# A stick-breaking attention whose joins move to GpSimd and whose value products change operands

## The reference

```python
proj = _rms(x, norm_g) @ w_in            # 1024 x 2048
q, g = split(proj)                       # 16 heads of 64
for each tile i of 128 queries, each head:
    z = q @ k.T / 8                      # masked to keys before the query
    a = exp(log_sigmoid(z) + reverse exclusive cumsum of log_sigmoid(-z))
    o = a @ v                            # 128 x 64
o = o * silu(g)
return x + o @ w_out
```

## Time and profile before

| | |
|---|---|
| median of 3 runs | 2390.4 us (2380.78 to 2392.75) |
| the profiled execution: its time | 2385.55 us |
| its span, first to last instruction | 2383.7 us |
| busy share PE, PEld, DVE, ACT, POOL | 97%, 52%, 67%, 43%, 9% |
| granted TensorE clock, mean | 0.997 of 2.4 GHz |
| second attention (first scan of query tile 0 to last value product) | 1980.8 to 2280.2 us |
| output product behind it | 2284.3 to 2383.7 us |

### The profile page before, as it was taken

One profiled execution on the slowest core, in us unless ns is written; L12 is line 12 of the kernel. 1 busy time (PEld: TensorE's weight loads), 2 busy tenths in 40 slices (PEclk: granted clock), 3 DMA queues, 4 the chain that ended last, 5 costly groups with the idle time before them and its releaser, 6 DMA issues.

```text
span 2383.7 us, 30315 instructions
## 1 busy us (share of the span) xinstructions
PE 2301.2 (97%) x12762; PEld 1234.2 (52%) x12762; DVE 1592.2 (67%) x2053; ACT 1017.9 (43%) x1482; POOL 208.1 (9%) x254
## 2 busy tenths in 40 slices
PE   7999999999999999999999988999999999989999
PEld 5445444444444444445544456654444446777765
DVE  6888867866766666787632389965534406989961
ACT  6255334322323223433322587732313216888841
POOL 0001030000000001623301100022000000000000
PEclk9999999999999999999999999999999999999999
DMA  5111010111110212103111000111231200010021
GB/s 187 36 37 69 1 36 36 61 46 71 58 49 36 71 71 71 38 1 142 36 71 36 32 5 1 62 46 36 71 141 36 72 1 1 1 36 1 1 89 54
DMA packets 50488, 116.02 MB, mean 49 GB/s; under 512 B 2418, under 2 KB 8107, under 8 KB 49968
## 3 DMA queue, kind: packets, MB, share of 16 engines
q1 hardware_dynamic: 48616, 105.40, 12.4%
q10 hardware_dynamic: 1736, 8.68, 0.9%
HBM read 101.49 MB, written 12.58 MB: 48 GB/s over the span
## 4 chain that ended last, share of the span: by engine, by line
PE 80%; DVE 11%; ACT 6%; issue 1%; DMA 1%; SPq 0%; DVEq 0%; ACTq 0%
PE PS L72 76%; PE PS L75 4%; ACT RG L81 3%; DVE R L93 2%; DVE RG L107 2%; ACT OV L84 2%; DVE R L101 1%; DVE RG L104 1%; DVE RG L101 1%; DVE RG L93 1%; ACT R L81 1%; DMA RG<-in_a_w_in 1%; DVE oss L110 1%; DVE dg L104 1%; DVE scl L110 0%
## 5 line engine op out<-in xcount | busy, mean ns | idle before, releaser
L72 PE MATMUL PS<-R,RG 128*128 128x512 f16 (+1 forms) x5184 | 1104.2, 374 | 9.4 <-DVE R L101 4.2
L72 PEld LDWEIGHTS PS<-R,RG 128*128 128x128 f16 (+1 forms) x5184 | 514.0, 104 | 592.8 <-issue 10.9
L72 PE MATMUL PS<-RG,R 128*128 128x512 f16 (+1 forms) x2904 | 631.2, 377 | 2.0 <-DVE R L101 1.7
L72 PEld LDWEIGHTS PS<-RG,R 128*128 128x128 f16 x2904 | 283.7, 98 | 330.0 <-issue 2.9
L81 ACT ACTIVATE RG<-RG,scl 128x4096 f16<-128x4096 f32 (+2 forms) x70 | 177.9, 2557 | 199.5 <-DVE scl L113 199.5
L101 DVE SCALAR_TENSOR_TENSOR RG<-RG,scl 128x4096 f16<-128x4096 f32 (+2 forms) x70 | 213.1, 3051 | 71.5 <-ACT RG L81 71.5
L101 DVE SCALAR_TENSOR_TENSOR R<-PS,scl,R 128x512 f32<-128x512 f32 (+1 forms) x227 | 159.2, 742 | 121.2 <-PE PS L72 98.8
L81 ACT ACTIVATE R<-PS,scl 128x512 f32<-128x512 f32 (+1 forms) x128 | 83.5, 685 | 326.4 <-PE PS L72 287.0
L107 DVE TENSOR_TENSOR_SCAN RG<-RG 128x127 f32<-128x127 f32 (+7 forms) x128 | 168.4, 1343 | 76.3 <-ACT RG L81 76.1
L110 DVE TENSOR_REDUCE scl<-RG 128x1 f32<-128x4096 f32 (+1 forms) x35 | 150.3, 4293 | 98.9 <-DMA RG<-in_w_ff 41.1
L72 PE MATMUL PS<-R,OV 128*128 128x64 f32 (+2 forms) x1456 | 193.7, 274 | 5.7 <-DVE R L93 5.4
(11 more groups left out here) (137 smaller groups left out, 1667.2 us busy)
## 6 DMA issues: line engine op xcount, KB each, us to landing
RG<-in_w_ff SPq DMA_DIRECT2D x16, 2048.0 KB, 8.5
RG<-in_a_w_in SPq DMA_DIRECT2D x8, 2048.0 KB, 8.7
xspill<-R ACTq DMA_DIRECT2D x2, 4096.0 KB, 16.0
RG<-in_w_kv SPq DMA_DIRECT2D x4, 2048.0 KB, 8.2
RG<-in_b_w_in SPq DMA_DIRECT2D x4, 2048.0 KB, 8.1
RG<-in_w_in SPq DMA_DIRECT2D x3, 2048.0 KB, 8.2
R<-in_x SPq DMA_DIRECT2D x8, 512.0 KB, 8.0
RG<-in_w_out SPq DMA_DIRECT2D x2, 2048.0 KB, 7.8
```

The lines of the kernel that those rows point to most:

```text
L72: return self.engine.matmul(*a, **k) if self.engine else Nothing()
```

## The change

- **Joins.** `tensor_tensor` of kept and beta moves from DVE's queue to POOL's, behind a new signal `scanned`; POOL no longer all-reduces the gates' peaks.
- **Value products.** V2 becomes stationary (64 columns), AT2 moving (128 columns). The result has features on partitions, odd heads on partitions 64 to 127, in the layout the output product wants of its stationary operand.
- **Gates.** All sixteen gate products become `product_t`, in the order `G2`; the last two, of tile 39, stay inside the attention.
- **Gate transposes** fall away: `gate_high` and `gate_low` read the gated values in SBUF (`gated_at`) and write HG, in the place of Q2. The bound of query tiles 0 to 6 comes from one PE matmul with ones (`gate_bound`) at u = N-1, that of tile 7 from another at (c, t) = (0, 1); splits of tiles 0 and 1 are issued inside the last steps of the attention.
- **Buffers.** `eb(u)` is in the raw buffer for u < 2, then in slot 0, so sigmoid of z waits for the peak of tile 40 at u = 0 and for the last gate product at u = 2. Tile 40 is loaded a second time, and its pieces move to u = 26 to 33. OUT moves to R2.

```diff
-        EB = [WS[:, 1024 * i:1024 * i + 1024] for i in range(4)]
+        def eb(u):
+            at = 1024 * u if u < 2 else 4096 + 1024 * (u % 4)
+            return RG[:, at:at + 1024]
         def kept(u):
-            return EB[2 + u] if u < 2 else EC[u % 3]
+            return EC[u % 3]
+        def gated_at(i, g):
+            return GATED[i // 4].rearrange("p (k t q) -> p k t q", k=8, t=4)[:, 4 * g:4 * g + 4, i % 4, :]
+        G2 = [("g2", c, mi, n) for n in range(2) for c in range(2) for mi in range(4)]
-        OUT = [R3[:, 1024 * i:1024 * i + 1024] for i in range(8)]
+        OUT = [R2[:, 1024 * i:1024 * i + 1024] for i in range(8)]
-        sb_pieces = range(22, 30)
+        sb_pieces = range(26, 34)
...
 # tensor
-            for t in range(NT - 1):
-                for c in range(2):
-                    product_n(38 + c, t, ("g2", t, c), bank=6 + c if t == NT - 2 else None)
+            for z, key in enumerate(G2[:14]):
+                _, c, mi, n = key
+                product_t(38 + c, mi, n, h_rhs, key, bank=z - 6 if z >= 12 else None)
+            def gate_bound(first, last, bank):
+                key = ("gate_bound", first)
+                b = banks.take_at(key, bank)
+                e.wait_ge(*sig("g_peak").at(last - 1))
+                e.wait_ge(*banks.free(key))
+                e.matmul(b[:, first:last], ones[:, :], col(24 + first, last - first), start=True,
+                         stop=True).then_inc(*full.up(*key))
...
-                            mm = e.matmul(banks.ap(("pvb", i, g))[:, 64 * (h % 8):64 * (h % 8) + 64],
-                                          AT2[v % 2][:, at:at + 128], V2[:, j, 64 * h:64 * h + 64],
-                                          start=(j == 0), stop=(j == i))
+                            r, q = 64 * (h % 2), 128 * (h % 8 // 2)
+                            mm = e.matmul(banks.ap(("pvb", i, g))[r:r + 64, q:q + 128], V2[:, j, 64 * h:64 * h + 64],
+                                          AT2[v % 2][:, at:at + 128], start=(j == 0), stop=(j == i))
...
-            gate_turn(0)
-            gate_turn(1)
             for c in range(2):
                 for t in range(NT):
+                    if (c, t) == (0, 1):
+                        gate_bound(7, 8, 7)
...
-                    e.wait_ge(*sig("bank_dve").at("gt", t, 1))
+                    e.wait_ge(*sig("g_low").at(t))
...
-                    if c == 0 and t + 2 < NT:
-                        gate_turn(t + 2)
 # vector
-                    scan.then_inc(*step.up())
-                if u < N:
-                    i, hs = sb_groups[u]
-                    w = width(i)
-                    eb, ec = by_head(EB[u % 4], u)[:, :, 0:w - 1], by_head(kept(u), u)[:, :, 1:w]
-                    e.wait_ge(*sig("beta").at(u))
-                    e.wait_ge(*step.last())
-                    e.tensor_tensor(eb, eb, ec, ALU.mult).then_inc(*sig("joined_b").up(u))
+                    scan.then_inc(*sig("scanned").up(u))
...
+                if u == N:
+                    gate_factors(0, 7)
+                    gate_low(0)
+                    gate_low(1)
 # scalar
                 if u < N:
-                    if u in (2, 3):
-                        e.wait_ge(*sig("joined_b").at(u - 2))
-                    if u >= 4:
+                    if u == 0:
+                        e.wait_ge(*sig("w_factor").at(40))
+                    if u == 2:
+                        e.wait_ge(*full.at(*G2[15]))
+                    if u >= 6:
                         e.wait_ge(*full.at("tb", u - 4, 1))
...
 # gpsimd
-            for i in range(NT):
-                e.wait_ge(*sig("g_peak").at(i))
-                across(col(32 + i), col(24 + i)).then_inc(*sig("g_top").up(i))
+            for u, (i, hs) in enumerate(sb_groups):
+                w = width(i)
+                beta, left = by_head(eb(u), u)[:, :, 0:w - 1], by_head(kept(u), u)[:, :, 1:w]
+                e.wait_ge(*sig("scanned").at(u))
+                e.wait_ge(*sig("beta").at(u))
+                e.tensor_tensor(beta, beta, left, ALU.mult).then_inc(*sig("joined_b").up(u))
             measure(41)
 # sync
-            for i in range(32, 42):
+            for i in range(32, 41):
                 load(i)
+            e.wait_ge(*sig("bank_full").at("tb", 1, 1))
+            e.dma_start(w_raw(40).rearrange("p (k n) -> p k n", k=8), w_source(40)).then_inc(
+                *sig("raw_again").up(by=16))
+            load(41)
```

More of the change, by code:

```diff
@@ L274, in tile_slot @@
                 return 2
[L275 removed]
+            return i % 3 if i < 40 else 41 - i
         def w_slot(i):
@@ L1014, in tensor @@
                     product_t(36 + c, mi, n, h_rhs, ("q2", c, mi, n), ready=h_ready("b_norm_2", n))
-            for t in range(NT - 1):
-                for c in range(2):
-                    product_n(38 + c, t, ("g2", t, c), bank=6 + c if t == NT - 2 else None)
-            def gate_turn(i):
-                for g in range(2):
-                    b = banks.take(("gt", i, g))
-                    e.wait_ge(*sig("g_gated").at(i, g))
-                    e.wait_ge(*banks.free(("gt", i, g)))
-                    for k in range(4):
-                        at = 512 * g + 128 * k
-                        mm = e.transpose(b[:, 128 * k:128 * k + 128], GG[:, i, at:at + 128], ident[:, :])
-                    mm.then_inc(*full.up("gt", i, g))
+            for z, key in enumerate(G2[:14]):
[8 more added lines that the diff above has]
+                         stop=True).then_inc(*full.up(*key))
             e.wait_ge(*sig("constants").at("mask_s"))
@@ L1067, in tensor @@
             scores([1])
-            product_n(38, NT - 1, ("g2", NT - 1, 0), bank=6)
+            product_t(39, 2, 1, h_rhs, G2[14], bank=6)
             scores([2])
-            product_n(39, NT - 1, ("g2", NT - 1, 1), bank=7)
+            product_t(39, 3, 1, h_rhs, G2[15], bank=7)
             for u in range(1, N + 2):
@@ L2063, in gate_low, with gate_factors @@
             def gate_low(i):
+                e.wait_ge(*sig("g_high").at(i, 1))
                 for g in range(2):
-                    key = ("gt", i, g)
-                    e.wait_ge(*sig("g_high").at(i, g))
-                    low_half(HT[:, i, g, 0, :, :], HT[:, i, g, 1, :, :],
-                             banks.ap(key).rearrange("p (k q) -> p k q", k=4), col(40 + i)).then_inc(
-                        *banks.empty([key], sig("bank_dve"), *key))
-            def gate_factor(i):
-                e.wait_ge(*sig("g_top").at(i))
-                power(col(63 + i), col(40 + i), col(32 + i)).then_inc(*sig("g_factor").up(i))
+                    up = sig("g_low").up(i) if g else step.up()
+                    low_half(HG[:, i, g, 0, :, :], HG[:, i, g, 1, :, :], gated_at(i, g), col(40 + i)).then_inc(*up)
+            def gate_factors(first, last):
+                key, n = ("gate_bound", first), last - first
+                e.wait_ge(*full.at(*key))
+                power(col(63 + first, n), col(40 + first, n), banks.ap(key)[:, first:last], key=key).then_inc(
+                    *sig("g_factor").up(first))
             N = len(sb_groups)
@@ L2118, in vector @@
                         *(sig("weight").up(40) if u - 1 == sb_pieces[-1] else step.up()))
-            for i in range(2):
-                gate_factor(i)
-                gate_low(i)
+                if u == N:
+                    gate_factors(0, 7)
+                    gate_low(0)
+                    gate_low(1)
             for c in range(2):
@@ L2734, in scalar, with gate @@
             e.dma_start(OV[:, 2048:2176], A["c_ms"]).then_inc(*sig("mask_in").up(by=16))
-            def gate_silu(t):
-                for c in range(2):
-                    key = ("g2", t, c)
-                    e.wait_ge(*full.at("g2", t, 1))
-                    e.wait_ge(*sig("w_scale").at(38 + c, 0))
-                    e.activation(GG[:, t, cols512(c)], banks.ap(key), ACT.Silu, scale=w_scale(38 + c)).then_inc(
-                        *banks.empty([key], sig("bank_act"), *key))
-            for t in range(NT - 1):
-                gate_silu(t)
+            def gate(key, function):
+                _, c, mi, n = key
+                e.wait_ge(*full.at(*key))
+                e.wait_ge(*sig("w_scale").at(38 + c, 0))
+                return e.activation(GT[n][:, 512 * (4 * c + mi):512 * (4 * c + mi) + 512], banks.ap(key), function,
+                                    scale=w_scale(38 + c))
+            for key in G2[:14]:
+                gate(key, ACT.Silu).then_inc(*banks.empty([key], sig("bank_act"), *key))
             def gate_high(i):
-                e.wait_ge(*sig("g_factor").at(i))
-                e.wait_ge(*full.at("gt", i, 1))
+                e.wait_ge(*sig("g_factor").at(0 if i < 7 else 7))
+                e.wait_ge(*full.at("zb", N - 1))
                 for g in range(2):
-                    key = ("gt", i, g)
-                    e.activation(HT[:, i, g, 0, :, :], banks.ap(key).rearrange("p (k q) -> p k q", k=4),
```

(4 more changed lines are left out.)

64 lines of the change are left out of this document (35 added, 29 removed).

## The result

The changed kernel takes 2413.18 us, median of 4 runs (2411.69 to 2414.72), beside 2390.66 for the kernel before in the same rounds: ratio 1.0102, 95% interval 1.0074 to 1.0131. It is slower, and the forecast of 2417 lies 4 us off. The profiled execution has a span of 2412.9 us, 29.2 more than before's 2383.7 (the forecast was +26.7), at the same mean granted clock, 0.997.

What follows compares the result with a forecast made beforehand. VectorE's queue, together with TensorE, was taken to set the pace from tile 2. Terms 27.2 + 8 + 1.1 + 1.1 - 10.7 = +26.7 on a median of 2390.4 give 2417 us; own range 2402 to 2446, stated range 2370 to 2446.

Steps and rivals of the forecast that it cites:

- Exclusion of scan and join: Attention: a VectorE scan with two SBUF sources and a GpSimd join block each other, so the pace is scan plus join.
- 27.2 floor: Attention, tiles 2 to 7: scan plus join sums to 292.2 against 265.0 us, +27.2 if the shared resource never idles.
- 8 idling: Attention: idle time of the resource shared by scan and join, taken as 3%, +8 us, bounds 0 and +24.
- 1.1 for the last join: End of the attention: the last join lies bare, 2.35 us for 1.22, +1.1 us.
- each less 0.14: Attention: with exclusion, scan and join each take their own length less 0.14 us.
- 4.8 for the low halves: Tiles 4 and 5: tile 40's 8 low halves, also with two SBUF sources, 8 x 0.60 = 4.8 us.
- Value products as nothing: TensorE, attention: 0 to 20 us gain from cheaper records against 33 us of shape changes; taken as 0, bounds -5 and +10.
- The tail, -10.7: Behind the attention: earlier start -3.6, fewer transposes -4.4, no wait at t = 6 -2.7; together -10.7 us, bounds -7 and -12.
- The wait at t = 6: Output stage: the product of t = 6 no longer waits 3.1 us behind tile 41's low half; -2.7 us.
- ScalarE's wait at u = 2, +1.1: Start of the attention: sigmoid of z waits for the last gate product, one sigmoid later; +1.1 us, 0 to 1.1.
- side by side: Rival, attention: scan and join overlap freely, since the scan holds nothing GpSimd needs; -21.5 us, 2369; chance 0.16.
- Side by side with the changes of shape: Rival, attention: scan and join overlap, but 128x64 shape changes make TensorE the bound; 2402 us; chance 0.10.

Runs made afterwards that it cites:

- e5: The changed kernel with each scan replaced by two reduces of the same columns with one SBUF source; 2397.99 us, ratio 1.0051.
- e1: The changed kernel with the joins alone put back on VectorE, 128x64 value products kept; 2393.81 us, ratio 1.0042.
- e6: The changed kernel with joins on VectorE and both heads' values as the 128x128 stationary operand; 2380.66 us, ratio 0.9972.
- e3: The changed kernel with the value products of the kernel before, joins still on GpSimd; 2426.79 us, ratio 1.0175.
- e12: The changed kernel with the old value products and one needless matmul per group ahead of the wait for the join; 2413.89 us, ratio 1.0127.
- e11: The changed kernel with joins on VectorE, odd heads first with 128x128 value products, tile 7's bound one product later; 2384.31 us, ratio 0.9994.
- e7: The changed kernel with the old value products and two needless matmuls per half group ahead of the wait for the join; 2440.81 us, ratio 1.0230.
- e8: The kernel before with tile 41 converted at (0, 5) instead of (0, 3); 2388.4 us, ratio 1.0009.
- e2: The kernel before with its joins moved to GpSimd and nothing else; 2430.15 us, ratio 1.0189.

## Why the prediction was right, and where two errors cancelled

**Exclusion of scan and join.** Right in mechanism, and shown by e5. What it is worth is 17.4 us.

**Attention +36.3 (27.2 floor, 8 idling, 1.1 for the last join): measured +36.4.** The idling was near; the floor came out right by two errors in opposite directions, which is luck. The price of a join, 2.35 us from the earlier trace rows, was too high: unstretched it is 2.00, 1.77, 1.54 and 1.32 us at 1023, 895, 767 and 639 columns. The rows it was taken from add another operand from another tensor. With these prices the prediction's own sum gives 8 x (1.62 + 1.40) + 8 x (2.16 + 1.86) = 56.3, 16 x (1.34 + 1.18 + 1.61 + 1.40) + 4.8 = 93.3 and 16 x (1.88 + 1.63 + 2.14 + 1.86) = 120.2, in all 269.8 instead of 292.2: a floor of +5. But "each less 0.14" holds for the scan alone. A join waits for its own scan and starts 0.08 us after it, so the pair takes 4.22 us in tile 7 and not 2.14 + 1.86 = 4.00 (the prediction, with the dear join, had 4.35), and of two scans of a group only the first is shortened. With the paces from join to join that the trace shows without further waits, 3.28 and 4.27 us a group in tiles 2 and 3, 2.74, 3.23, 3.73 and 4.22 in tiles 4 to 7, the floor is 283.1 us, 287.9 with the prediction's 4.8 for the low halves: +23. The 1.1 us for the last join was counted twice, as the floor has that join already.

What is left, 301.1 less 287.9, is 13.2 us of idling, where 8 with bounds 0 and 24 had been taken. It doesn't lie in the late groups: tile 7 takes 68.7 us for 16 x 4.22 = 67.5, and 8.4 of the 13.2 us are in tile 4. There VectorE waits for ScalarE up to 4.5 us at a time, and TensorE was at 1.2 GHz from 2075.1 to 2078.5, where eight records of a half group took 1.97 instead of 1.09 us. How much of the 8.4 us this explains is open. The loop that the prediction named (scan u+1 waits for ScalarE, which waits for a copy behind join u-1) is there, but it mostly delays a scan that would stand still anyway.

**Value products as nothing, bounds -5 and +10.** The gain of 0 to 20 us isn't there: a half group's eight weight loads are shorter with a 64-column operand, 0.85 against 0.97 us, but its eight products are not, 1.09 against 1.06. The changes of shape cost 0.11 to 0.13 us each where 0.10 had been read from the earlier trace rows, with 0.17 us of idle time ahead of each load. The Trainium skill, TensorEngine Tiling (Array Packing), "Key Properties", says that a change of mode drains the engine, and the trace agrees with that idle time. What the changes do to the time depends on who sets the pace. With the joins on VectorE the exchanged operands cost 15.3 us (e1), 12.1 of them by the shape and 3.2 in e6's form. With the joins on GpSimd nearly nothing: in the tiles at full clock e3 and e12 are 0 to 1.0 us shorter than after. So nothing was the right term for this change, and the reason given, that TensorE has time to spare at the new pace, fits. It is also why undoing the joins gives back only 21.1 of the 36.4 us: moved joins without the narrow products make all of the loss where the clock is kept (e12), the changed operands alone 15.3, and the first covers the second.

**The tail, -10.7: measured -7.9.** Start earlier: -2.4 for -3.6, counted from the last join. The early splits are in the way of the attention's last copy on ScalarE, for which TensorE waits 0.49 us, and the first product then waits 0.29 us for VectorE's last `gated`; the prediction had the splits early and at no cost. The rest of the 1.2 us is not traced. Eight transposes fewer: as said, products follow each other every 5.62 us. The wait at t = 6: gone, as worked out. A further 1.4 us is a step that the prediction left out: it looked at the order of the new small matmul, not at the bank it is put in. e11 gets it back.

**ScalarE's wait at u = 2, +1.1:** +0.7 by the first scan of tile 2. **Rivals:** side by side falls with e5's contrast; even if it had held, e5 shows that the time would have been near 2398, not 2369. That the 128x64 products then set the pace is argued and not shown. Side by side with the changes of shape was the better sum (2402) for a mechanism that isn't so.

**Clock.** The prediction had no term of it, and after hardly needs one: 3.4 us at 1.2 GHz in the attention. But that is luck: the same kernel with slightly less work on TensorE (e3) lies 14 us higher. That the drops make most of this difference is shown by e12 for the attention, with e7's tiles 4 and 7 beside it, and e8 against before gives a price in the same code, 4.0 us for tile 4 at 0.90. How much of e3's and e2's medians it makes in all is open, as e12's fillers cost something too and its clock fell in other places.

## What to carry to other kernels

Before work is moved to an idle engine, look whether it can run beside what it is moved away from: a scan with both sources in SBUF and a GpSimd `tensor_tensor` take turns, and each handover between them is paid on top. Ask of each of the two whether it can start beside the other at all: the scan could, and gained 0.13 us; the join, which reads its own scan's result, could not. And don't trust a sum because it comes out right: here a price 17% too high made up for a saving that wasn't there. A result layout that saves eight transposes later isn't free if it changes the array's shape twice in every half group; a wider stationary operand with a useless half was faster than the narrow one.

## What the runs showed of the hardware that I had not expected

- A float32 `tensor_tensor` on GpSimd, in place, 1023 columns: 2.00 us, against 2.35 for 1024 columns with another operand.
- A scan of 1023 columns that began beside such a join ended 2.14 or 2.15 us after the join, whenever it began, in 13 of 13 cases; alone it takes 2.28. VectorE work with one SBUF source (`gated`, reduces) kept its time beside joins, and so did the joins.
- A stationary operand of 128x64 gives no shorter products than 128x128 here (281 and 276 ns a record); each change of shape around them costs 0.11 to 0.13 us.
- TensorE's granted clock fell to 1.2 GHz in stretches of e2 and e3, where it had waited for GpSimd's joins (58 us of e3's 312), and a useless matmul in each group was worth more than it cost (attention 312.2 to 301.4 us).
